# Attention over two heads at a time in a four-layer block: zero-padded keys, one list of head pairs per layer, fewer passes in stick-breaking

## The chip, the cores and the metric

One core of one Trainium2 chip runs the whole program in one launch. The metric is device microseconds of that core: 2575.2 as the median of three runs (2564.73 to 2580.36). One execution was profiled; it took 2568.69 us, and the span from its first to its last instruction is 2566.9 us.

Words used below: TensorE does matrix products (PE in rows; its weight loads are PEld), VectorE is DVE, ScalarE is ACT, GpSimd is POOL, SyncE is SP. A matrix product takes a stationary operand (up to 128 rows by 128 columns) and streams a moving operand through it. A float32 product is recorded as two matmuls, a transpose as one.

## The reference

256 tokens of width 1024 pass through two blocks of two layers. All arithmetic is float32. The parts that the change touches are the attentions of three of the layers. In the first layer eight heads do stick-breaking attention and eight do dilated attention; for 256 tokens the dilated branches come together in one bias row per head:

```python
z = jnp.einsum('bqhd,bkhd->bhqk', q_blk, k) * scale
causal = k_pos[None, :] < (start + jnp.arange(Q_BLOCK))[:, None]
log_keep = jnp.where(causal, jax.nn.log_sigmoid(-z), 0.0)
later = lax.cumsum(log_keep, axis=3, reverse=True) - log_keep
log_w = jnp.where(causal, jax.nn.log_sigmoid(z) + later, -jnp.inf)
return jnp.einsum('bhqk,bkhd->bqhd', jnp.exp(log_w), v)
```

The third layer has three softmax attentions over 256 keys (selected blocks, window, block mixture, here "moba"; eight heads of width 64 each), the fourth has one of four heads of width 128 + 64 ("mla") and one of eight heads of width 64 with a sink ("sliding"). Each of them is

```python
s = jnp.einsum('bkgqd,bksd->bkgqs', qb, k_w) * scale + bias
p = e / (jnp.sum(e, axis=-1, keepdims=True) + ...)   # e = exp(s - max)
o = jnp.einsum('bkgqs,bksd->bkgqd', p, v_w)
```

Everything else (feed-forward, mixture of experts, mLSTM, projections) stays as it is.

## The kernel before

The program is a list of stages (`STAGES`), and each engine walks through the list with its own function for each kind of stage. Between most stages all engines drain and wait for each other (`boundary`); stages in `JOINED` run into each other, the softmax attentions of one layer among them. Inside a stage the order on each engine is the order of the code, and semaphores with constant counts tie the engines together. Nothing is planned or reordered.

Weights come in pieces of 1 MB into a ring of five buffers, issued by SP. ACT rounds each piece to a high part (`high_part`), DVE subtracts it to get the low part, and TensorE does three products for each. The first one or two pieces of the stage after next are split `early`, inside the attention.

Queries and keys lie transposed in `big`, two heads to a block of 256 columns: one head in rows 0 to 63, the other in rows 64 to 127. A head's scores are causal, so for the first 128 queries only 128 keys are computed and for the second 128 queries all 256: 384 columns for each head, in `wide[:, 0, h, :]`.

**Softmax attention** (`soft_attention`), for each head h, one after the other:
- TensorE: two float32 products of 64 rows, 128 and 256 columns moving, into bank h % 2 (line 847 in rows, since all products go through one helper); three transposes of the exponentials (line 1052); three products with the values (64 columns moving, stationary `PT`).
- DVE (`biased_scores`, lines 2038 and 2042): scale and bias for 384 columns out of the bank, then the row maximum of each query tile; later the copy of the transposed exponentials out of the bank to `PT[h % 2]` (line 2056).
- ACT: two exponentials with their row sums (line 1633).

On TensorE's queue head h's transposes come first, then the scores of head h + 2, then the values of head h - 1. At the end of a stage DVE divides by the sums (and multiplies by the gates) out of banks 4 and 5 into `nrm`; where the next stage is an attention too, its first two heads' scores are biased before that.

**Stick-breaking** (`stick`) keeps the scores of a head the other way round (keys on partitions). For eight heads each: DVE copies the scores out of the bank; ACT does Abs and Exp, and after the eighth head Ln; DVE then does three passes over 384 columns (max and add; subtract; multiply by the strict causal mask), all 24 before it does anything else; TensorE sums over later keys with a constant triangle and a block of ones (`later`: 256, 128 and 128 columns moving); DVE subtracts, ACT exponentiates, DVE multiplies by the mask again, and TensorE multiplies with the values.

Of the kernel before, what the change touches and what calls it, by code (L numbers as in the profile page):

```python
# [38 lines left out]
ALU = mybir.AluOpType  # L39
# [43 lines left out]
C_MINCL = C_MSTRICT + W3  # L83
# [12 lines left out]
def shape_constants():  # L96
# [3 lines left out]
    for at, mask in ((C_MSTRICT, j > p), (C_MINCL, j >= p)):  # L100
# [40 lines left out]
def build(nc, I, out):  # L141

    ctx = ExitStack()
    with ctx:
# [83 lines left out]
        p_read = sem("p_read")  # L228
# [123 lines left out]
        def wide_at(at, n):  # L352
# [9 lines left out]
        S_RW, S_R = 232, 360  # L362

# [19 lines left out]
        QA, KA, VA, QD, KD, VD = (1024 * i for i in range(6))  # L383
        M_PRE, M_V = 0, 4096
        (N_Q, N_KC, N_VC, N_KS, N_VS, N_KW, N_VW, N_QB, N_KB, N_VB) = (
            0, 1024, 1280, 1536, 1792, 2048, 2304, 2560, 3584, 4608)
# [12 lines left out]
        def t2(at, scale=1.0):  # L399
            return [("TT", 0, 256, big[:, at:at + 512], scale)]  # L400

# [13 lines left out]
        def gview(at):  # L415
# [3 lines left out]
            "attn": [t2(QA, 0.125), t2(QA + 512, 0.125), t2(KA), t2(KA + 512), n256(VA, 512, 0), n256(VA, 512, 1),  # L419
                     t2(QD, 0.125), t2(QD + 512, 0.125), t2(KD), t2(KD + 512), n256(VD, 512, 0), n256(VD, 512, 1)],  # L420
# [6 lines left out]
                     [("T", 0, P, big_t(N_KS, 0), 1.0), n1(big_n(N_VS, P), P)],  # L427
                     [("T", 0, P, big_t(N_KW, 0), 1.0), n1(big_n(N_VW, P), P)],
                     [n1(gview(S_G))],
                     t2(N_QB, 0.125), t2(N_QB + 512, 0.125), t2(N_KB), t2(N_KB + 512),  # L430
# [3 lines left out]
                    [("T", 0, P, big_t(O_K, 0), 1.0), n1(big_n(O_V, P), P)]],  # L434
# [7 lines left out]
        def pair_heads(qat, kat):  # L442

            def parts(h):
                p0 = 64 * (h % 2)
                return [(big[p0:p0 + 64, qat + (h // 2) * T:qat + (h // 2 + 1) * T],
                         big[p0:p0 + 64, kat + (h // 2) * T:kat + (h // 2 + 1) * T])]
            return parts

        def group_heads(qat, kat):  # L450

            def parts(h):
                p0, g = 64 * (h // 4), h % 4
                return [(big[p0:p0 + 64, qat + g * T:qat + (g + 1) * T], big[p0:p0 + 64, kat:kat + T])]
            return parts

        def mla_heads(h):
            qrT = aux[0:64, A_QRT + h * T:A_QRT + (h + 1) * T]
            return [(big_t(O_QNT, h), big_t(O_KNT, h)), (qrT, aux[0:64, A_KRT:A_KRT + T])]
# [3 lines left out]
        def soft(parts, v, heads, dv, dst, bias=True, scale=1.0, pad=None, gate=None):  # L463
            return dict(parts=parts, v=v, heads=heads, dv=dv, dst=dst, bias=bias, scale=scale, pad=pad, gate=gate)

        SOFT = {
            "dilated": soft(pair_heads(QD, KD), lambda h, t: big_n(VD, 512)[:, t, 64 * h:64 * h + 64], H, 64, 512),
            "selected": soft(group_heads(N_Q, N_KS), lambda h, t: big_n(N_VS, P)[:, t, 64 * (h // 4):64 * (h // 4) + 64],
                             H, 64, 0, gate=1),
            "window": soft(group_heads(N_Q, N_KW), lambda h, t: big_n(N_VW, P)[:, t, 64 * (h // 4):64 * (h // 4) + 64],  # L470
                           H, 64, 0, gate=2, pad=S_PAD),
            "moba": soft(pair_heads(N_QB, N_KB), lambda h, t: big_n(N_VB, 512)[:, t, 64 * h:64 * h + 64], H, 64, 512),
# [6 lines left out]
        for spec in SOFT.values():  # L479
            spec["head0"], spec["step0"], spec["steps"] = at, steps, 3 if spec["pad"] is None else 5  # L480
            at, steps = at + spec["heads"], steps + spec["heads"] * spec["steps"]
# [1913 lines left out]
```

## Time and profile before

| | |
|---|---|
| median of three runs | 2575.2 us |
| profiled execution | 2568.69 us, span 2566.9 us |
| TensorE busy, share of the span | 2257.0 us, 88% |
| mean granted TensorE clock | 0.893 of full speed |
| stick-breaking (first score product to last copy) | 311.6 to 358.7 us |
| dilated attention | 358.8 to 391.2 us |
| selected, window, moba | 1393.2 to 1488.3 us |
| mla, sliding | 2033.1 to 2090.0 us |

The stages are told apart by the lines of their rows. The granted clock is shown as a share of 2.4 GHz; two levels occur, 1.0 and 0.5 (1.2 GHz). A row of the view by stretches gives each engine's busy time and count, then the clock and the DMA share.

### The profile page before, as it was taken

The page shows a single profiled execution, that of the slowest core. Times are in us where ns is not written, and L with a number is a line of the kernel's source. Part 1 is how long each engine was busy: PE and PEld are TensorE (multiplying, and loading weights), DVE is VectorE, ACT ScalarE, POOL GpSimd, SP SyncE. Part 2 cuts the span into 40 slices and gives each one's busy share as a digit, 9 for nine tenths or more (in the row PEclk, how much of TensorE's full clock was granted, in tenths as well). Part 3 has the DMA queues.
Part 4 walks back from the last instruction along what each step waited for, and adds up shares of the span by engine and source line. Part 5 has one row for each costly group of instructions (what it writes and reads, how often), then busy time and mean ns, then how long its engine had stood idle before and what let it go on. Part 6 is the DMA issues. An engine that isn't in the chain of part 4 may idle for free.

```text
span 2566.9 us, 31115 instructions
## 1 busy us (share of the span) xinstructions
PE 2257.0 (88%) x13152; PEld 1966.7 (77%) x13152; DVE 1731.5 (67%) x1455; ACT 1067.0 (42%) x1078; POOL 694.8 (27%) x340
## 2 busy tenths in 40 slices
PE   7997968998998955899897977999997886999996
PEld 6897957997997954899795666877776675877775
DVE  5896355997998446699622556777776256777766
ACT  4433434334334324333321234555553223555554
POOL 2996002995996000499300000000000000000000
PEclk9998958998999976999896578999998777999998
DMA  9775504776776530578551004887775203777873
GB/s 331 262 266 202 174 1 145 269 264 216 264 264 219 165 100 9 197 259 281 185 154 60 1 30 160 302 284 272 276 266 174 66 1 116 254 270 266 297 259 145
DMA packets 281915, 495.91 MB, mean 193 GB/s; under 512 B 11816, under 2 KB 167576, under 8 KB 281744
## 3 DMA queue, kind: packets, MB, share of 16 engines
q1 hardware_dynamic: 257952, 410.13, 47.7%
q0 software_dynamic: 23552, 82.75, 9.0%
q8 instruction: 104, 1.70, 0.3%
q10 hardware_dynamic: 272, 1.05, 0.1%
q14 instruction: 35, 0.29, 0.0%
HBM read 486.50 MB, written 12.10 MB: 194 GB/s over the span
## 4 chain that ended last, share of the span: by engine, by line
PE 75%; DVE 13%; DMA 5%; ACT 4%; issue 2%; DVEq 0%; ACTq 0%; SPq 0%
PE psum L847 73%; DVE low L1757 3%; DMA ring<-in_moe_w_up 3%; ACT wh L1440 2%; DVE nrm L1757 1%; PE psum L1052 1%; DMA ring<-in_ffn_w_up 1%; DVE wide L1757 1%; PE psum L904 1%; DVE xl L1757 1%; DMA ring<-in_ffn_w_gate 1%; DVE wide L2126 1%; DVE hl L1757 1%; DVE nrm L1816 1%; DVE nrm L1991 1%
## 5 line engine op out<-in xcount | busy, mean ns | idle before, releaser
L1757 DVE TENSOR_TENSOR low<-ring,wh 128x2048 fp32r<-128x2048 f32 x386 | 1075.8, 2807 | 371.2 <-ACT wh L1440 369.1
L1440 ACT ACTIVATE wh<-ring 128x2048 fp32r<-128x2048 f32 x386 | 733.4, 1906 | 691.8 <-PE psum L847 282.0
L847 PE MATMUL psum<-xh,wh 128*128 128x256 f32 x1832 | 523.6, 286 | 20.3 <-DVEq L580 18.5
L847 PE MATMUL psum<-xh,low 128*128 128x256 f32 x1832 | 524.4, 286 | 0.0
L847 PE MATMUL psum<-xl,wh 128*128 128x256 f32 x1832 | 521.9, 285 | 0.0
L847 PEld LDWEIGHTS psum<-xh,wh 128*128 128x128 f32 x1832 | 354.4, 193 | 26.6 <-DVEq L580 20.9
L665 POOL TENSOR_TENSOR big<-big 128x1024 f32<-128x1024 f32 x144 | 366.8, 2547 | 11.3
L847 PEld LDWEIGHTS psum<-xl,wh 128*128 128x128 f32 x1832 | 353.3, 193 | 1.6
L847 PEld LDWEIGHTS psum<-xh,low 128*128 128x128 f32 x1832 | 353.4, 193 | 0.0
L847 PE MATMUL psum<-wh,xh 128*128 128x256 f32 (+5 forms) x864 | 279.3, 323 | 14.2 <-DVEq L580 8.8
L847 PE MATMUL psum<-wh,xl 128*128 128x256 f32 (+5 forms) x864 | 276.0, 319 | 0.0
L847 PE MATMUL psum<-low,xh 128*128 128x256 f32 (+5 forms) x864 | 275.8, 319 | 0.0
L847 PE MATMUL psum<-wh,hh 128*128 128x512 f32 x672 | 268.3, 399 | 7.7 <-DVE low L1757 7.7
L847 PE MATMUL psum<-wh,bigr 128*128 128x512 f32 x768 | 251.7, 402 | 16.6 <-DVE hl L1757 16.6
L847 PE MATMUL psum<-wh,hl 128*128 128x512 f32 x672 | 266.0, 396 | 0.0
L847 PE MATMUL psum<-low,hh 128*128 128x512 f32 x672 | 265.9, 396 | 0.0
L634 POOL DMA_DIRECT2D gain<-adaln_parts x12 | 6.4, 538 | 879.6 <-DVE nrm L1757 827.5
L665 POOL TENSOR_TENSOR big<-big,ccol 128x2048 f32<-128x2048 f32 x48 | 195.9, 4081 | 40.4 <-DMA big<-in_ada_w 39.3
L847 PEld LDWEIGHTS psum<-wh,xh 128*128 128x128 f32 x864 | 169.2, 196 | 27.6 <-DVEq L580 10.8
L847 PEld LDWEIGHTS psum<-wh,bigr 128*128 128x128 f32 x768 | 145.8, 190 | 55.0 <-DVE low L1757 21.9
L847 PEld LDWEIGHTS psum<-wh,xl 128*128 128x128 f32 x864 | 168.8, 195 | 11.9
L847 PEld LDWEIGHTS psum<-low,xh 128*128 128x128 f32 x864 | 169.6, 196 | 10.7
(318 smaller groups left out, 2645.5 us busy)
## 6 DMA issues: line engine op xcount, KB each, us to landing
ring<-in_moe_w_gate SPq DMA_DIRECT2D x64, 1024.0 KB, 5.2
ring<-in_moe_w_up SPq DMA_DIRECT2D x64, 1024.0 KB, 5.3
ring<-in_moe_w_down SPq DMA_DIRECT2D x64, 1024.0 KB, 5.0
big<-in_ada_w POOLq DMA_DIRECT2D x48, 1024.0 KB, 6.6
ring<-in_ffn_w_gate SPq DMA_DIRECT2D x44, 1024.0 KB, 5.4
ring<-in_ffn_w_up SPq DMA_DIRECT2D x44, 1024.0 KB, 5.7
ring<-in_ffn_w_down SPq DMA_DIRECT2D x44, 1024.0 KB, 5.2
ring<-in_mlstm_w_in SPq DMA_DIRECT2D x16, 1024.0 KB, 5.6
```

The source lines that it names most:

```text
L634: pool.dma_start(gain[k % GAINBUFS][:, :], src).then_inc(gain_in[k % GAINBUFS], 16)
L665: pool.tensor_tensor(out_, a, b, op).then_inc(ada_step, 1)
L847: return pe.matmul(out_, lhsT, rhs, start=start, stop=stop, **kw)
L904: last = pe.transpose(psum[:, q, i * P:(i + 1) * P], nrm[:, t, f:f + P], ident)
L1052: last = pe.transpose(psum[:, 2 + h % 2, i * P:(i + 1) * P], wide[:, 0, h, i * P:(i + 1) * P], ident)
L1440: act.activation(wh[n % PARTS][:, 0:w], ring[n % RING][:, 0:w], ACT.Copy).then_inc(high, 1)
L1757: return dve.tensor_tensor(out_, a, b, op)
L1816: ins = dve.scalar_tensor_tensor(out=nrm[:, t, :], in0=x[:, t, :], scalar=stat[:, t:t + 1], in1=gain[g % GAINBUFS][:, :], op0=ALU.mult, op ...
L1991: ins = dve.scalar_tensor_tensor(out=nrm[:, t, :], in0=y, scalar=stat[:, t:t + 1], in1=factor, op0=ALU.mult, op1=ALU.mult)
L2126: dve.scalar_tensor_tensor(out=cv[:, m, tap:T], in0=src[:, 0:T - tap], scalar=w, in1=cv[:, m, tap:T], op0=ALU.mult, op1=ALU.add)\
```

## The change

Two heads are handled together everywhere in the attentions.

- **Padded keys.** ACT writes the transposed keys (for stick-breaking the queries) of two heads into a tile of 512 columns: head one in rows 0 to 63 of the first 256 columns, head two in rows 64 to 127 of the second 256, zeros elsewhere. GpSimd writes the zeros (`pad_keys`) when the projection stage begins. Such a projection piece takes two ACT copies of 64 partitions instead of one of 128 (kind "Z"). One float32 product with the stationary queries of both heads on 128 rows then gives the scores of both heads: 512 columns moving for the second query tile, 256 for the first.
- **Pairs.** DVE biases both heads in two operations (512 and 256 elements in each row) and takes the maxima in two. ACT does four exponentials for a pair, then itself copies the first head's transposed exponentials to `PT[0]`; DVE copies the second's to `PT[1]`. TensorE's order is: six transposes of the pair, scores of the pair after next, values of the pair.
- **One list per layer.** Selected, window and moba become one stage, mla and sliding one; scores of the next attention start while the last pairs of the previous one run. Maxima and sums have two sets of columns that alternate. The division of an attention follows on DVE behind the biasing of the pair after next.
- **Early pieces.** ACT splits them before the exponentials of the last pair (before: behind the fourth head of eight), DVE behind the last copy, as before.
- **Stick-breaking.** The strict mask is added to the scores as 0 or -1e30 when they leave the bank, so both multiplications by the mask go. The triangle now includes the diagonal, so the separate subtraction goes. Copies, Abs, Exp, Ln and max-and-add work on two heads (768 elements).

```diff
+    c[:, C_MSTRICT:C_MSTRICT + P] = (j > p)[:, :P]
+    for at, mask in ((C_STICK, np.where(j > p, 0, NEG)), (C_MINCL, j >= p)):
...
-    c[:, C_AFTER:C_AFTER + P] = p > j[:, :P]
+    c[:, C_AFTER:C_AFTER + P] = p >= j[:, :P]
...
+        def pair_heads(qat, keys):
+
+            def products(p, t):
+                q, n = big[:, qat + p * T + t * P:qat + p * T + (t + 1) * P], (t + 1) * P
+                return [(0, 2 * n, q, padded(keys, p)[:, :, 0:n], True, True)]
+            return products
...
-                for name in ("selected", "window", "moba"):
-                    add("soft", name)
+                add("soft", ("selected", "window", "moba"))
...
+            def pad_keys(tile):
+
+                tile = tile.rearrange("p (n h t) -> p n h t", h=2, t=T)
+                for half in range(2):
+                    pool.memset(tile[64 * half:64 * half + 64, :, 1 - half, :], 0.0).then_inc(zeroed, 1)
...
+                for i, pair in enumerate(run):
+                    turn_probs(*pair, 0)
+                    turn_probs(*pair, 1)
+                    if i + 2 < len(run):
+                        scores_read(*pair)
+                        scores(*run[i + 2])
+                    values(*pair, 0)
+                    values(*pair, 1)
...
+                        elif kind == "Z":
+                            n = m // P
+                            both_ = dst.rearrange("p (j h t) -> p j h t", j=n, h=2)
+                            src = psum[:, b, at:at + n * T].rearrange("p (j t) -> p j t", j=n)
+                            act.activation(both_[0:64, :, 0, :], src[0:64], ACT.Copy, scale=scale)
+                            dst, src = both_[64:P, :, 1, :], src[64:P]
...
+                for i, (name, p) in enumerate(run):
+                    a = SOFT[name]
+                    j = a["pair0"] + p
+                    act.wait_ge(biased, a["step0"] + a["steps"] * (p + 1))
+                    for h in a["pair"](p):
+                        for t, (lo, hi) in ((1, (P, W3)), (0, (0, P))):
...
+                    act.wait_ge(p_turned, 2 * j + 1)
+                    if j:
+                        act.wait_ge(headout, 2 * j - 1)
+                    act.activation(PT[0][:, :], psum[:, 2, 0:W3], ACT.Copy).then_inc(p_read_act, 1)
...
+                    if i == len(run) - 2:
                         for j, shape in enumerate(early(s + 2)):
                             high_part(PIECE0[s] + j, shape)
...
             def stick(s, k):
 
+                for p in range(H // 2):
+                    dve.wait_ge(stick_pe, p + 1)
+                    for lo, hi, bank in ((0, T, p % 2), (T, W3, 6 + p % 2)):
+                        tt(wide[:, 0, 2 * p:2 * p + 2, lo:hi],
+                           psum[:, bank, 0:2 * (hi - lo)].rearrange("p (h w) -> p h w", h=2),
+                           spread(const[:, C_STICK + lo:C_STICK + hi], 1, 2), ALU.add).then_inc(stick_dve, 1)
+                for p in range(H // 2):
+                    z, sp = (wide[:, i, 2 * p:2 * p + 2, :] for i in range(2))
+                    dve.wait_ge(stick_act, p + 1)
+                    dve.scalar_tensor_tensor(out=sp, in0=z, scalar=0.0, in1=sp, op0=ALU.max, op1=ALU.add)\
+                        .then_inc(stick_dve, 1)
                 for h in range(H):
-                    dve.wait_ge(stick_pe, h + 1)
-                    dve.tensor_copy(wide[:, 0, h, :], psum[:, h % 2, 0:W3]).then_inc(stick_dve, 1)
-                for h in range(H):
-                    z, sp_h = wide[:, 0, h, :], wide[:, 1, h, :]
-                    at = H + 3 * h
-                    dve.wait_ge(stick_act, h + 1)
-                    mark(dve.scalar_tensor_tensor(out=sp_h, in0=z, scalar=0.0, in1=sp_h, op0=ALU.max, op1=ALU.add),
-                         stick_dve, at + 1)
-                    mark(tt(z, z, sp_h, ALU.subtract), stick_dve, at + 2)
-                    mark(tt(sp_h, sp_h, const[:, C_MSTRICT:C_MSTRICT + W3], ALU.mult), stick_dve, at + 3)
...
+                for i, (name, p) in enumerate(run):
+                    j = SOFT[name]["pair0"] + p
+                    dve.wait_ge(p_turned, 2 * j + 2)
+                    if j:
+                        dve.wait_ge(headout, 2 * j)
+                    dve.tensor_copy(PT[1][:, :], psum[:, 3, 0:W3]).then_inc(p_read_dve, 1)
+                    if i + 2 < len(run):
+                        biased_scores(*run[i + 2])
+                    if i == len(run) - 1:
+                        for j, shape in enumerate(early(s + 2)):
+                            low_part(s, PIECE0[s] + j, shape)
+                    if p == SOFT[name]["pairs"] - 1:
+                        scaled_values(name)
```

**TensorE in the middle of the dilated attention.** Before, two heads (`PT0` and `PT1` are the transposed exponentials; `psum<-big` without `PT` are scores, `psum<-const,wide` transposes):

```order
L1052 MATMUL psum<-const,wide 128x128 x3
L847 MATMUL psum<-big 128x128
L847 MATMUL psum<-big 128x256
L847 MATMUL psum<-big,PT0 128x64 x3
L1052 MATMUL psum<-const,wide 128x128 x3
L847 MATMUL psum<-big 128x128
L847 MATMUL psum<-big 128x256
L847 MATMUL psum<-big,PT1 128x64 x3
```

Now, the same work of one pair:

```order
L1094 MATMUL psum<-const,wide 128x128 x6
L889 MATMUL psum<-big 128x512
L889 MATMUL psum<-big 128x256
L889 MATMUL psum<-big,PT0 128x64 x3
L889 MATMUL psum<-big,PT1 128x64 x3
```

Four score products have become two of double width; transposes and values are as many as before, and each kind stands together.

**DVE in stick-breaking.** Before (the triple of lines 2017 and 1757 stands eight times):

```order
L2012 COPY wide<-psum 128x384 x8
L2017 SCALAR_TENSOR_TENSOR wide<-wide 128x384
L1757 TENSOR_TENSOR wide<-wide 128x384
L1757 TENSOR_TENSOR wide<-wide,const 128x384
...
L1757 TENSOR_TENSOR wide<-wide,psum 128x384 x8
L1757 TENSOR_TENSOR wide<-wide,const 128x384 x8
```

Now (the first two rows stand four times):

```order
L1818 TENSOR_TENSOR wide<-psum,const 128x2x256
L1818 TENSOR_TENSOR wide<-psum,const 128x2x128
...
L2080 SCALAR_TENSOR_TENSOR wide<-wide 128x768 x4
L1818 TENSOR_TENSOR wide<-wide,psum 128x384 x8
L2100 SCALAR_TENSOR_TENSOR wide<-psum,biasT 128x2x256
L2100 SCALAR_TENSOR_TENSOR wide<-psum,biasT 128x2x128
```

Of the 24 operations between the logarithms and the subtractions four are left, and none stands between the subtractions and the values.

**ACT at the end of the dilated attention.** Now, the last two pairs (`wh1<-ring0` is the early high part):

```order
L1696 ACTIVATE PT0<-psum 128x384
L1486 ACTIVATE wh1<-ring0 128x2048
L1691 ACTIVATE wide,small<-wide,small 128x256
L1691 ACTIVATE wide,small<-wide,small 128x128
L1691 ACTIVATE wide,small<-wide,small 128x256
L1691 ACTIVATE wide,small<-wide,small 128x128
L1696 ACTIVATE PT0<-psum 128x384
```

The high part stands ahead of the last pair's four exponentials; before it stood ahead of the fifth head's.

## Rows read from the trace of the kernel before

**Rows 1.** Page, busy time of each engine and share of the span.

```profile
PE 2257.0 (88%) x13152; PEld 1966.7 (77%) x13152; DVE 1731.5 (67%) x1455; ACT 1067.0 (42%) x1078; POOL 694.8 (27%) x340
```

**Rows 2.** By stretches: length, busy PE, PEld, DVE, ACT, POOL, then PEclk, DMA.

```profile
340.30:343.90 3.60, 3.60 (x13) 3.23 (x14) 0.86 (x2) 1.39 (x3) 0.00 (x0) 0.50 0.00 0
344.10:347.70 3.60, 3.60 (x24) 3.25 (x23) 2.19 (x4) 1.83 (x4) 0.00 (x0) 1.00 0.02 5
348.90:350.80 1.90, 1.90 (x17) 1.90 (x18) 1.90 (x5) 0.00 (x0) 0.00 (x0) 1.00 0.00 0
...
358.80:391.20 32.40, 27.93 (x104) 20.82 (x104) 18.23 (x36) 9.69 (x33) 0.00 (x0) 0.50 0.00 1
391.30:394.90 3.60, 3.60 (x16) 3.22 (x16) 1.55 (x3) 1.79 (x3) 0.00 (x0) 0.50 0.00 0
395.30:396.30 1.00, 0.00 (x0) 0.00 (x0) 0.82 (x2) 0.26 (x1) 0.00 (x0) 1.00 0.00 0
...
1393.20:1488.30 95.10, 86.44 (x312) 64.66 (x312) 56.12 (x131) 25.69 (x98) 0.00 (x0) 0.50 0.00 1
...
2033.20:2050.70 17.50, 17.39 (x46) 10.42 (x47) 5.79 (x14) 4.43 (x14) 0.00 (x0) 0.51 0.00 0
2051.10:2054.10 3.00, 3.00 (x16) 2.97 (x15) 1.20 (x3) 0.41 (x2) 0.00 (x0) 0.50 0.00 0
2054.20:2060.90 6.70, 4.07 (x26) 2.92 (x25) 4.43 (x13) 1.97 (x8) 0.00 (x0) 1.00 0.00 0
2061.00:2090.00 29.00, 23.52 (x89) 17.98 (x86) 19.99 (x46) 9.62 (x27) 0.00 (x0) 0.50 0.00 1
```

**Rows 3.** Timeline of TensorE in the dilated attention: start, length, what.

```profile
373.64 1.65 PE L847 MATMUL psum<-big 64*128 64x128 f32 x4
375.22 1.54 PE L847 MATMUL psum<-big,PT 128*128 128x64 f32 x6
376.55 0.85 PE L1052 MATMUL psum<-const,wide 128*128 128x128 f32 x3
...
377.33 1.65 PE L847 MATMUL psum<-big 64*128 64x128 f32 x4
```

**Rows 4.** Timeline of TensorE where the sliding attention begins.

```profile
2055.07 1.57 PE L847 MATMUL psum<-big 64*128 64x128 f32 x8
...
2058.92 0.55 PE L1052 MATMUL psum<-const,wide 128*128 128x128 f32 x3 [2.27 <-ACT wide L1633]
```

**Rows 5.** Timeline of TensorE: transposes of two heads in a row of mla.

```profile
2040.48 0.90 PE L1052 MATMUL psum<-const,wide 128*128 128x128 f32 x3
...
2044.76 0.90 PE L1052 MATMUL psum<-const,wide 128*128 128x128 f32 x3
```

**Rows 6.** Timeline of stick-breaking, ACT, DVE and TensorE.

```profile
324.71 4.15 ACT L1619 ACTIVATE wide<-wide,const 128x384 f32<-128x384 f32 x8
325.36 0.56 DVE L2017 SCALAR_TENSOR_TENSOR wide<-wide 128x384 f32<-128x384 f32 x1 [7.01 <-ACT wide L1619]
...
340.29 7.46 PE L847 MATMUL psum<-wide,const 128*128 128x256 f32 x36 [9.53 <-DVE wide L1757]
...
357.62 1.09 ACT L1625 ACTIVATE nrm<-psum 128x512 f32<-128x512 f32 x2 [8.72 <-PE psum L847]
```

**Rows 7.** Groups by form, dilated attention: busy, mean ns of one.

```profile
L2038 DVE SCALAR_TENSOR_TENSOR wide<-psum,biasT 128x384 f32<-128x384 f32 x8 | 4.5, 558 | 18.3 <-PE psum L847 18.3
...
L1633 ACT ACTIVATE wide<-wide,small 128x256 f32<-128x256 f32 x8 | 3.9, 492 | 0.0
L2042 DVE TENSOR_REDUCE small<-wide 128x1 f32<-128x256 f32 x8 | 3.4, 420 | 0.3
...
L1757 DVE TENSOR_TENSOR low<-ring,wh 128x2048 fp32r<-128x2048 f32 x1 | 2.3, 2282 | 0.0
L1440 ACT ACTIVATE wh<-ring 128x2048 fp32r<-128x2048 f32 x1 | 1.9, 1893 | 0.0
L1757 DVE TENSOR_TENSOR nrm<-psum,small 128x512 f32<-128x512 f32 x2 | 1.3, 687 | 0.0
```

More of the change, by code:

```diff
@@ L461, in build, with soft @@
         vmla = big_n(O_KVM, 1024).rearrange("p t (h w) -> p t h w", h=MH)
-        def soft(parts, v, heads, dv, dst, bias=True, scale=1.0, pad=None, gate=None):
-            return dict(parts=parts, v=v, heads=heads, dv=dv, dst=dst, bias=bias, scale=scale, pad=pad, gate=gate)
+        def soft(products, pair, v, heads, dv, dst, bias=True, scale=1.0, pad=None, gate=None):
+            return dict(products=products, pair=pair, v=v, heads=heads, pairs=heads // 2, dv=dv, dst=dst, bias=bias,
+                        scale=scale, pad=pad, gate=gate)
@@ L473, in build @@
-            "mla": soft(mla_heads, lambda h, t: vmla[:, t, h, P:2 * P], MH, P, 0, bias=False, scale=192.0 ** -0.5),
-            "sliding": soft(group_heads(O_Q, O_K), lambda h, t: big_n(O_V, P)[:, t, 64 * (h // 4):64 * (h // 4) + 64],
+            "dilated": soft(pair_heads(QD, big[:, KD:KD + 2048]), next_to,
+                            lambda h, t: big_n(VD, 512)[:, t, 64 * h:64 * h + 64], H, 64, 512),
+            "selected": soft(group_heads(N_Q, big[:, N_KS:N_KS + 512]), across,
+                             lambda h, t: big_n(N_VS, P)[:, t, 64 * (h // 4):64 * (h // 4) + 64], H, 64, 0, gate=1),
@@ L478, in build, with pairs_of @@
         at, steps = 0, 0
-        for spec in SOFT.values():
-            spec["head0"], spec["step0"], spec["steps"] = at, steps, 3 if spec["pad"] is None else 5
-            at, steps = at + spec["heads"], steps + spec["heads"] * spec["steps"]
+        for i, spec in enumerate(SOFT.values()):
+            spec["index"], spec["pair0"], spec["step0"], spec["steps"] = i, at, steps, 4 if spec["pad"] is None else 5
+            spec["nmx"], spec["sum"], spec["inv"] = (S_SOFT[i % 2] + 16 * j for j in range(3))
+            at, steps = at + spec["pairs"], steps + spec["pairs"] * spec["steps"]
+        def pairs_of(names):
+            return [(name, p) for name in names for p in range(SOFT[name]["pairs"])]
         STAGES = []
@@ L1075, in gates @@
+                pe.wait_ge(zeroed, {"dilated": 4, "selected": 8, "mla": 10}[names[0]])
+                scores(*run[0])
+                scores(*run[1])
+                for i, pair in enumerate(run):
[6 more added lines that the diff above has]
+                    values(*pair, 1)
             def gates(s, k):
@@ L1622, in stick @@
+                for p in range(H // 2):
+                    sp = wide[:, 1, 2 * p:2 * p + 2, :]
+                    act.activation(sp, sp, ACT.Ln, bias=ones).then_inc(stick_act, 1)
+                for h in range(H):
+                    act.wait_ge(stick_dve, H + H // 2 + h + 1)
                     act.activation(wide[:, 0, h, :], wide[:, 0, h, :], ACT.Exp).then_inc(stick_act, 1)
-                act.wait_ge(stick_pe, 2 * H + 1)
+                act.wait_ge(stick_pe, H // 2 + H + 1)
                 for t in range(TT):
@@ new lines, in biased_scores @@
+                ha, hb = a["pair"](p)
+                hs = slice(ha, hb + 1, hb - ha)
+                nmx = small[:, a["nmx"]:a["nmx"] + 16].rearrange("p (h t) -> p h t", t=TT)
+                dve.wait_ge(score, j + 1)
+                tiles = ((1, P, W3, j % 2), (0, 0, P, 6 + j % 2))
+                for t, lo, hi, bank in tiles:
+                    add = biasT[:, hs, lo:hi] if a["bias"] else spread(const[:, C_CAUSAL + lo:C_CAUSAL + hi], 1, 2)
+                    dve.scalar_tensor_tensor(out=wide[:, 0, hs, lo:hi],
+                                             in0=psum[:, bank, 0:2 * (hi - lo)].rearrange("p (h w) -> p h w", h=2),
+                                             scalar=a["scale"], in1=add, op0=ALU.mult, op1=ALU.add).then_inc(biased, 1)
```

289 lines of the change are left out of this document (135 added, 154 removed).

## The prediction

> **What bounds the kernel now.** I read the page first: TensorE is busy for 88% of the span and no other engine comes near [rows 1], so only a change that shortens TensorE's work, speeds its clock or fills its gaps counts. Then the view by stretches. The three softmax stages and stick-breaking (47.1 us from first product to last copy) take 231.6 of 2566.9 us. In the dilated stage TensorE is busy for 27.93 of 32.40 us, in the third layer's for 86.44 of 95.10, and the granted clock is 0.50 in both from end to end, that is 1.2 GHz; DVE is busy for 18.23 and 56.12 [rows 2]. So these stages are bound by a TensorE at half speed. In the timeline a head takes 3.69 us (373.64 to 377.33): 1.58 for the scores, 1.33 for the values, 0.78 for the transposes, handovers included [rows 3].
>
> **Why the clock is low.** Rises follow stretches in which products on 128 rows stand back to back: `later` ran 3.60 us at 0.50 and then 3.60 at 1.00; the 16 transposes behind the dilated stage ran at 0.50, and the next microsecond, with no matmul in it, already has 1.00; mla's last values and transposes (128 rows, 3.00 us full) at 0.50 are followed by 6.70 us at 1.00 [rows 2]. The stages of 64-row scores never rise, although TensorE is as busy, and even mla, whose scores are half 128 and half 64 rows, stays at 0.51 for 17.50 us with 17.39 busy. So rows count, and transposes count. Values (64 columns per load) kept 1.00 right behind `later` for the 1.90 us shown.
>
> The Trainium skill, page "TensorE: Matmul & The Clock Gate", speaks against this twice. Its section on the HAM clock gate lets the clock follow how busy TensorE has been; by that alone padding to 128 rows changes nothing. This trace disagrees: 86.44 of 95.10 us busy never lifted the clock. Its Part 4 says that transposes do not count as busy. This trace disagrees here too (the 16 transposes). By the page the softmax stages would stay at half speed, which is rival B.
>
> **The change part by part**, from the bottom up.
>
> *One pair at full clock.* Scores: as many columns as two heads have now, and those took 1.57 us at 1.00 [rows 4]. Values: 17 records in 1.90 us, 0.112 each [rows 2]; 12 make 1.34. Transposes: 0.55 for three [rows 4], three more at 0.112: 0.88. One further handover, 0.1. Sum 3.9 us, where two heads take 7.37 now. *At half clock:* scores 2 x 1.58, values 2 x 1.33, transposes 2 x 0.78 [rows 3], less a handover of some 0.3 saved at two places: 6.9. Which clock holds: six transposes and the scores of a pair now stand together, all on 128 rows, 4.2 us at half speed with one handover in it, as in the stretches after which it rose. Once up, a pair has its 128-row work in 3.8 of 3.9 us. I take full clock.
>
> *Do DVE and ACT keep up with 3.9?* DVE for a pair: bias 0.69 (512 elements as in the division) and about 0.43, maxima 0.69 and 0.42, a copy of 0.56 [rows 7]: 2.8. ACT: four exponentials, at most 0.49 each [rows 7], and the copy, 0.52 by the logarithms' 4.15 / 8 [rows 6]: 2.5 to 3. Yes, in both cases; the waiting work (bias of pair i + 2 behind the copy of pair i) has almost a whole period before it is needed. The padded attentions add some 0.35 on DVE; it still fits.
>
> *Fill and tail.* First transposes of a stage end after its first scores (1.6), bias and maxima (2.2), exponentials (2.0) and transposes (0.4): 6.2. Behind the last transposes: copy 0.56, early low part 2.28, division 2 x 0.69 [rows 7], small steps and waits 0.4: 4.6, as today. New on the path: the early high part, 1.89 [rows 7], stands ahead of the last pair's exponentials; about 0.5 is covered, so +1.4.
>
> *Dilated*, four pairs: 6.2 + 3 x 3.9 + 1.4 + 4.6 = 23.9, and 0.9 for a start that may still be at half clock: 24.8 for 32.4. **-7.6.**
>
> *Selected, window, moba*, twelve pairs: 6.2 + 11 x 3.9 + 1.4 + 4.6 = 55.1. First scores start at half clock: +0.7. At two crossings DVE divides and gates (four operations of 0.69 and small ones, 3.2) before it copies for the next pair; its slack is 1.1: +2.1 each. Sum 60.0 for 95.1. **-35.1.** The crossings themselves cost now too (their gain is in the 95.1).
>
> *mla, sliding* (2033.1 to 2090.0, 57 us). An mla head takes 4.28 from transposes to transposes, 3.8 of it scores [rows 5]: they still have 64-row halves. Both mla pairs' scores now come first: 4 x 3.8 = 15.2, at half clock. Then transposes, sliding's first scores and mla's values, all on 128 rows: 7.0 at half clock, the clock rising on the way: 5.6. The second such group at full clock: 4.0. Three periods of sliding 11.7 (the last two without scores: -0.6), its transposes 0.7; two high parts on ACT: +3.0; tail with two low parts and the sink's steps: 7.2. Sum 46.8. **-10.2.**
>
> *Stick-breaking.* The first logarithm starts at about 324 as now: four pairs of Abs and Exp at 2 x 0.87 (0.52 for 384 elements; 768 by the slope to 1.89 for 2048 [rows 6, 7]) save 1.9, wider scores and mask additions give 1.0 of it back. Then today 24 operations (first at 325.36) stand ahead of the subtractions, and `later` runs from 340.29 [rows 6]. Now four of 0.96 do, and `later` starts at 325.7 and can run through: about 2.4 heads at 1.71 (half clock, twice 0.925) until the clock rises, 5.6 at 0.925 (today 3.60 us for 3.9 heads [rows 2]): 9.2, to 334.9. Values follow at once, without the mask pass: 48 records, 5.4 at full clock; today 8.7. End 340.6, copies 1.1 [rows 6]: 341.7 for 358.7, -17.0. If the clock falls in the values they take 10.2, and it is -12.2. I take **-16.5**.
>
> *At nothing or nearly.* GpSimd's zeros: its queue stands empty of urgent work when a projection begins, and the first scores come over 60 us later in both large stages; price if the cover goes, a few us once. The second copy of a padded piece: 0.6 on ACT, which has 2.5 us of work per projection piece against over 5 on TensorE; only the last piece of the fourth layer shows: +0.5.
>
> Sum: -7.6 - 35.1 - 10.2 - 16.5 + 0.5 = -68.9. From the profiled 2568.7: 2499.8. That execution lies 6.5 us under the median of 2575.2 and inside the three runs' own spread; I forecast **2500 us**, 2.9% less than the median.
>
> **Rivals.**
>
> *A. The clock holds only in part, or handovers are dearer* (a pair takes 5.2). For it: mla rose late and fell back when 64-row scores and waits came [rows 2]; crossings leave TensorE waiting for 2 us. Against: the 128-row share of a pair. 22 pairs x 1.3 = +28.6: 2528. 12%.
>
> *B. The clock stays at 0.50 in the softmax stages* (the zeros, or the page's rule). Against it: the moving operand of the 16 transposes is the identity, nearly all zeros, and it lifted the clock. 22 x (7.37 - 6.9) = 10 less fills and the high parts, some 6; stick-breaking -13 to -16.5: 2548. 10%.
>
> *C. Slower than before: the pair turns serial.* ACT now carries exponentials and a copy, and the copy of pair i waits for transposes that wait for its own exponentials; if nothing overlaps at half clock, a pair is 2.0 (exponentials) + 1.3 + 0.9 (copies) + 2.9 + 2.7 = 9.8. 22 x 2.4 = +53, less 16.5: 2605. It decides from a pair of 7.37 + 16.5 / 22 = 8.1 us on. Against: scores of pair i + 2 lie between the transposes and values on TensorE's queue and need nothing fresh. 3%.
>
> *Forecast*, 75%: 2484 (pairs at 3.6, handovers wholly hidden, and the values at full clock) to 2515 (values at half clock, every fill a few us longer).
>
> The range takes the forecast's and most of A: **2482 to 2534**. A change of 1% (25.8 us) is about what can be told here; B lies on that line (2549.4), so half of it is "same": faster 0.92, same 0.05, slower 0.03.
>
> **What the changed profile would show.** The clock at 1.00 from the second pair of each softmax list on; scores starting every 3.9 us in the dilated stage; DVE's two copies no longer behind 24 passes, `later` starting near 326; the third layer's attention at about 60 us. The forecast is wrong if the stretches of 128-row scores still read 0.50, or if TensorE waits on ACT's copy (line 1696) in every pair.

## The result, and the profile after

The changed kernel takes **2495.3 us** (median of four runs, 2489.99 to 2501.18) against 2573.4 (four runs): a ratio of 0.970, 95% interval 0.966 to 0.973. The forecast was 2500 and its range 2482 to 2534, so the result lies inside. The profiled execution took 2491.27 us, its span 2489.5 at a mean granted clock of 0.922; before it was 2566.9 at 0.893. One line of the page answers to [rows 1]:

```profile
PE 2186.2 (88%) x13056; PEld 1909.5 (77%) x13056; DVE 1692.1 (68%) x1337; ACT 1075.1 (43%) x1097; POOL 703.5 (28%) x350
```

TensorE lost 70.8 us of busy time with only 96 fewer matmuls, so most of it is the same work at another speed. The view by stretches has the four attention stages (stick-breaking, dilated, selected to moba, mla and sliding) and the first score products of mla alone; the columns are those of [rows 2]:

```profile
312.25:342.81 30.56, 20.63 (x113) 16.93 (x113) 12.00 (x20) 19.27 (x25) 0.00 (x0) 0.83 0.11 35
342.81:365.79 22.98, 16.84 (x88) 12.51 (x89) 13.56 (x24) 10.63 (x37) 0.00 (x0) 0.84 0.00 1
...
1366.74:1423.98 57.24, 47.64 (x264) 36.23 (x264) 40.22 (x83) 29.09 (x110) 0.00 (x0) 0.86 0.00 1
1965.79:2009.93 44.14, 36.06 (x156) 25.27 (x156) 22.90 (x45) 18.98 (x58) 0.00 (x0) 0.70 0.00 1
1965.79:1980.47 14.68, 14.68 (x33) 7.85 (x34) 1.94 (x4) 3.15 (x9) 0.00 (x0) 0.51 0.00 1
```

The clock was 0.50 throughout the dilated and the third layer's attention before, and 0.50 in mla and sliding but for one stretch of 6.7 us; now it is 0.84, 0.86 and 0.70. The timeline of TensorE in the dilated stage (start, length, what) answers to [rows 3]:

```profile
353.00 0.83 PE L1094 MATMUL psum<-const,wide 128*128 128x128 f32 x6
353.66 1.46 PE L889 MATMUL psum<-big 128*128 128x512 f32 x4
354.95 1.45 PE L889 MATMUL psum<-big,PT 128*128 128x64 f32 x12
356.23 0.82 PE L1094 MATMUL psum<-const,wide 128*128 128x128 f32 x6
...
359.98 0.55 PE L1094 MATMUL psum<-const,wide 128*128 128x128 f32 x3 [1.12 <-ACT wide L1691]
```

From one pair's transposes to the next it is 3.23 us. The last row shows the last pair: its transposes wait 1.12 us for exponentials, which stand behind the early high part on ACT. Stick-breaking, against [rows 6], ACT's logarithms and then TensorE's sums and values:

```profile
324.59 3.41 ACT L1674 ACTIVATE wide<-wide,const 128x768 f32<-128x768 f32 x4
...
326.57 9.74 PE L889 MATMUL psum<-wide,const 128*128 128x256 f32 x48 [8.73 <-DVE wide L2080]
336.14 5.47 PE L889 MATMUL psum<-big,wide 128*128 128x64 f32 x48
```

The first of the two crossings in the third layer, in the chain of waits:

```profile
1380.80 2.58 PE psum L889 x16
1383.38 0.66 PE psum L1094 x6
1384.04 1.31 PE psum L889 x4
...
1385.37 1.02 DVE wide L2100 x2
1386.39 0.93 DVE small L2105 x2
...
1390.82 1.52 PE psum L889 x12
```

The chain leaves TensorE for DVE (biasing, maxima, the division and gating) and comes back at 1390.82. Then the clock is gone for a while; TensorE's timeline at the same place:

```profile
1390.82 1.52 PE L889 MATMUL psum<-big,PT 128*128 128x64 f32 x12 [2.25 <-DVE nrm L1818]
...
1392.90 2.76 PE L889 MATMUL psum<-big 128*128 128x512 f32 x4
```

The scores that took 1.46 take 2.76: the granted clock is 0.50 from 1392.77 to 1396.18. The second crossing looks the same, with a wait of 2.46 and scores of 2.77.

By stages, each from its transposes of the normed tokens to the next: projection, stick-breaking and dilated 157.12 to 131.71, the third layer's 231.85 to 193.98, the fourth's 133.33 to 121.34. These are 75.3 of the 77.4 us that the span lost. All others move by less than 2.3 us, but for the last (the second mixture of experts and the end), whose instructions are the same: 435.34 before, 439.63 after.

### The profile page after: what moved, and what is told of

It reads as the page before. It is cut to its first block, busy times and chain, and to the rows that moved or that the text cites. A ratio compares the mean times of both kernels' runs of the same rounds, so it can differ in the third digit from the quotient of the medians.

```text
span 2489.5 us, 30826 instructions
## 1 busy us (share of the span) xinstructions
PE 2186.2 (88%) x13056; PEld 1909.5 (77%) x13056; DVE 1692.1 (68%) x1337; ACT 1075.1 (43%) x1097; POOL 703.5 (28%) x350
## 4 chain that ended last, share of the span: by engine, by line
PE 75%; DVE 12%; DMA 5%; ACT 4%; issue 2%; DVEq 1%; ACTq 0%; SPq 0%
PE psum L889 73%; DVE low L1818 3%; DMA ring<-in_moe_w_up 3%; ACT wh L1486 2%; DVE nrm L1818 1%; DMA ring<-in_ffn_w_up 1%; DVE xl L1818 1%; DVE wide L2188 1%; DMA ring<-in_ffn_w_gate 1%; PE psum L946 1%; DVE hl L1818 1%; DVE nrm L1877 1%; PE psum L1094 1%; DVE nrm L2052 1%; DVEq L611 0%
```

## The experiments

**Theory T**: products on 128 rows lift the granted clock, and this is most of the gain in the softmax stages. **Rival P**: pairing and the joined list keep TensorE fed, and that is the gain. In stick-breaking, T holds DVE's queue of passes responsible. "Stage" below is the length by the same marks as just above, which the profile of each kernel gives. In the first two kernels the scores are not those of the heads, as their expectations say; their order and shapes are what is compared.

### Pairs, but 64 rows (e1_rows64, e1_again)

```diff
-                return [(0, 2 * n, q, padded(keys, p)[:, :, 0:n], True, True)]
+                return [(i * n, i * n + n, q[0:64], padded(keys, p)[0:64, 0, 0:n], True, True)
+                        for i in range(2)]
```

> The changed kernel, but the scores of a pair of heads come from two products on 64 rows each instead of one on 128 (the same columns, the same order, pairs and lists; the second head of a pair gets the first head's keys and queries, so its scores are the wrong ones). Theory T (the 128 rows lift the clock, and the clock is most of the gain): the granted clock of the dilated stage and of the third layer's attention reads 0.50 through most of it, a pair takes 6.3 to 6.9 us instead of 3.24; 18 pairs by about 3.3 is +60 (mla and sliding +5 at most): 2550 to 2565 us. Rival P (pairing, fewer operations and the joined list give the gain, and the clock would rise for any TensorE kept this busy): the clock stays at 1.00 and the time within 10 us of the changed kernel's 2495.

Measured: 2521.2 us (ratio to before 0.981, 0.979 to 0.983). By stretches, the third layer's attention, and TensorE's chain in it:

```profile
1373.52:1459.00 85.48, 82.97 (x312) 71.23 (x313) 40.70 (x83) 28.89 (x110) 0.00 (x0) 0.50 0.00 1
```

```profile
1400.75 1.28 PE psum L1096 x6
1402.03 5.61 PE psum L891 x20
1407.63 1.28 PE psum L1096 x6
```

In this layer T holds where it spoke of the clock: 0.50 from end to end, and 6.89 us a pair; the dilated attention reads 0.53. TensorE was busy for 82.97 of 85.48 us, a larger share than in the changed kernel (47.64 of 57.24), and it stayed at half speed. P falls. The Trainium skill, page "TensorE: Matmul & The Clock Gate", Part 1, lets the clock follow how busy TensorE has been recently; the measurement disagrees again, and it decides.

My figure for the whole was wrong: 2550 to 2565 expected. The stage of the third layer costs +28.2 (222.22), the dilated one +5.9, where eleven and three periods of 3.65 more would be 40 and 11. I had forgotten what the changed kernel pays and this one doesn't: TensorE stands idle for 2.5 us in this attention against 9.6, so at 6.89 a pair most of DVE's work at a crossing and of ACT's high part is hidden, and a clock that is low cannot fall. And 13 us lay elsewhere: the last stage, untouched, took 426.61 instead of 439.63. So I ran the same kernel again:

> The kernel with two 64-row products for a pair's scores once more, for its last stage alone: it took 426.61 us without one drop of the clock. If that belongs to the program, it is 427 again and the whole about 2520; if it is chance, 435 to 445 and the whole 2530 to 2538.

It took 2529.97 (one execution). The third layer's stage is 222.25, within 0.03 us of the first execution, and the dilated one 137.07 (137.59). The fourth layer's does not repeat, 117.11 against 128.03, nor does the last stage, 440.76; more on it below.

The fourth layer also shows where T stops. Its sliding attention has 64-row scores in this kernel too, and there they ran at full clock (the second execution):

```profile
2020.35:2033.50 13.15, 12.83 (x95) 11.33 (x93) 10.59 (x26) 8.36 (x29) 0.00 (x0) 1.00 0.01 1
```

```profile
2024.04 0.82 PE L1096 MATMUL psum<-const,wide 128*128 128x128 f32 x6
2024.79 1.57 PE L891 MATMUL psum<-wide,big 64*128 64x256 f32 x8
2026.43 1.52 PE L891 MATMUL psum<-big,PT 128*128 128x64 f32 x12
2027.79 0.82 PE L1096 MATMUL psum<-const,wide 128*128 128x128 f32 x6
```

A pair takes 3.75 us here, not 6.89. The clock had been at 1.00 since 1993.46, through mla; in the first execution it rose in the middle of this list, at 2027.51. So rows decide the clock in the dilated and the third layer's attention, but 64-row scores as such do not rule out full speed. What is different in the fourth layer was not tried.

### One head at a time, but 128 rows (e2_before_rows128)

```diff
-                p0 = 64 * (h % 2)
-                return [(big[p0:p0 + 64, qat + (h // 2) * T:qat + (h // 2 + 1) * T],
-                         big[p0:p0 + 64, kat + (h // 2) * T:kat + (h // 2 + 1) * T])]
+                return [(big[:, qat + (h // 2) * T:qat + (h // 2 + 1) * T],
+                         big[:, kat + (h // 2) * T:kat + (h // 2 + 1) * T])]
```

> The kernel before, one head at a time, but the scores of a head in dilated, selected, window, moba and sliding come from a product on all 128 rows of the two heads' block (so each holds the sum of two heads' scores; same columns, same number of instructions, no zeros needed). Theory T: rows alone lift the clock; the stages go to 1.00, a head then takes 2.0 us by TensorE and up to 2.3 where DVE or ACT (three operations and two exponentials a head) are slower, instead of 3.7: the third layer's attention 95 falls to 55 to 65, dilated 32.5 to 21 to 25; time 2505 to 2530 us. Rival P (pairs are needed, because the handovers inside a head keep the clock down): clock 0.50, 2565 to 2580 us.

Measured: 2530.0 us (0.984, 0.982 to 0.985), at the upper end; the third layer's attention, 70.10, lies above the 55 to 65 expected. The dilated attention and the third layer's:

```profile
359.55:382.68 23.13, 16.66 (x105) 13.11 (x105) 17.84 (x36) 9.57 (x33) 0.00 (x0) 0.93 0.00 1
1384.53:1454.63 70.10, 53.30 (x313) 43.30 (x313) 55.16 (x131) 25.57 (x98) 0.00 (x0) 0.84 0.00 1
```

Rows alone bring the dilated attention from 32.47 to 23.13; the changed kernel has 22.98. In the third layer they bring 25.0 of the 37.9 us. This is the cleanest experiment on T: order, columns and counts are those of the kernel before, and only the rows differ. Of the 12.9 us that are missing in the third layer, DVE has a part: it is busy for 55.16 of 70.10 us (40.22 in pairs), and TensorE waits for its copy of the transposed exponentials 12 times, 7.6 us in all. The joined list, which this kernel lacks, has another; the two are not told apart here. Pairs and list without rows (the kernel above) are worth 9.6. So the two parts together give 3.3 us more than their sum.

### Without the crossings (e8_no_crossing)

```diff
-                    if i + 2 < len(run):
+                    if i + 2 < len(run) and run[i + 2][0] == pair[0]:
...
+                    if i + 2 < len(run) and run[i + 1][0] != pair[0]:
+                        scores_read(*pair)
+                        scores(*run[i + 1])
+                        scores(*run[i + 2])
```

(and the same on DVE: biasing of the next two pairs, then the division).

> The changed kernel without the crossing of attentions: the first two score products of the next attention stand behind the last values of the one before, and DVE biases its first two pairs and then divides, as in the kernel before. If the joined list is worth what I put it at (a crossing costs 2.1 us instead of a fill of 6.2 and a division): 4 to 6 us more at each of the three crossings, and the clock falls in each gap: +12 to +22 in all, the third layer's attention at 66 to 72 us. Rival (the list is worth little, since the crossings already stop TensorE for 2 us and cost the clock): under +6.

Measured: 2503.8 us, +8.5; the third layer's stage 200.40, +6.4 for two crossings. Neither forecast is met: +12 to +22 was too much, under +6 too little. TensorE's timeline behind the last pair of an attention:

```profile
1390.20 0.55 PE L1094 MATMUL psum<-const,wide 128*128 128x128 f32 x3 [2.03 <-ACT wide L1695]
...
1394.49 1.52 PE L889 MATMUL psum<-big,PT 128*128 128x64 f32 x12 [1.57 <-DVE nrm L1822]
```

A fill here is a wait of 2.03 and one of 1.57, and the scores between are at full clock. I had gone by the 6.2 of a fill from a stage's start, but the scores in it are work that is due in either order. Counted from the start of the list, the seventh pair's transposes come 1.5 us later than in the changed kernel, so this crossing costs 1.5 more. The second costs the other 4.9; there the clock is 0.50 for 10.2 us, from 1410.32 on, against 3.4 in the changed kernel. So the rival had part of the reason (a crossing already costs a wait and some clock), and what a fill costs hangs on whether the clock falls.

### What a crossing and the high part cost (e3_adds_later, e4_high_early, e5_both)

```diff
-                        link(tt(part, y, f, ALU.mult))
-                        dve.wait_ge(scaled, 2 * a["index"])
-                        tt(o, o, part, ALU.add).then_inc(scaled, 1)
+                        tt(part, y, f, ALU.mult).then_inc(scaled, 1)
...
+                    if p < TT and i > p and SOFT[run[i - p - 1][0]]["gate"] is not None:
+                        added_values(run[i - p - 1][0], p)
```

> The changed kernel, but where one gated attention hands over to the next DVE only multiplies out of banks 4 and 5 at once; the two additions to nrm (0.69 each) follow behind the biasing of the next two pairs. Theory T (the wait of 2.25 us ahead of the values at 1390.82 is DVE's queue: biasing, four passes of 0.69, then the copy): the wait falls by 1.4 us at each of the two crossings of the third layer, to about 0.8, and if the clock then does not fall behind it (2.76 us for scores that take 1.46), another 1.5 each: that layer's attention 57.2 falls to 51 to 54.5; -3 to -6 in all. Rival (the additions only move: they delay the copy of a later pair by as much): within 1 us.

The third layer's stage fell from 193.98 to 187.67, -6.3, a little more than expected. At the first crossing:

```profile
1387.18 1.46 PE L889 MATMUL psum<-big 128*128 128x512 f32 x4
1389.43 1.52 PE L889 MATMUL psum<-big,PT 128*128 128x64 f32 x12 [0.79 <-DVE wide L1818]
1390.79 0.82 PE L1094 MATMUL psum<-const,wide 128*128 128x128 f32 x6
1391.45 1.46 PE L889 MATMUL psum<-big 128*128 128x512 f32 x4
```

The wait is 0.79 instead of 2.25 (1.00 instead of 2.46 at the second crossing), and the next scores take 1.46 instead of 2.76. Two additions of 0.69 taken off the path of each crossing paid twice, since the clock did not fall. The program as a whole took 2494.4 us, no better than the changed kernel: the first mixture of experts, also untouched, took 431.98 instead of 424.94.

```diff
-                    if i == len(run) - 2:
+                    if i == 0:
```

> The changed kernel, but ACT splits the early weight pieces behind the first pair of a list instead of ahead of the last pair's exponentials. Theory T (the high part of 1.9 us holds up the last pair: a gap of 1.1 us before its transposes in the dilated stage): -1.1 in dilated and about as much in the third layer, -2 to -3 in the fourth where it is 3.7 us; -4 to -6 in all. Rival (ACT is no freer in the first pair, and the high part delays the second pair's exponentials instead; or DVE's low part and the division set the end anyway): within 1 us, or up to +2.

2492.0 us, -3.3 by the medians where 4 to 6 less were expected. The third layer's stage is -1.2, as expected. The dilated one (with its projection and stick-breaking) is 130.28 instead of 131.71, but the unchanged program came to 130.29 when it ran again (below), so the stage decides nothing. The dilated attention alone takes 21.24 against 22.98 and 22.70; but it took 21.40 in the kernels without crossings and with eight masks, which leave it as it is. So only the wait that is gone is shown, not what it is worth in time. In the fourth layer the whole stage says nothing either (118.01, against 121.34 and 117.62 unchanged), but the list from its first transposes on does: 27.59, and 27.58 and 27.59 in the two executions below, where five executions with the old order took 29.53 to 30.47. Its last pair, in the changed kernel and then here:

```profile
2001.15 1.78 PE L1094 MATMUL psum<-const,wide 128*128 128x128 f32 x6 [2.87 <-ACT wide L1691]
```

```profile
2001.76 1.05 PE L1094 MATMUL psum<-const,wide 128*128 128x128 f32 x6
```

> Both of these edits, additions later and high parts early. If both theories hold: the dilated stage 22 us, the third layer's attention 50 to 53.5, mla and sliding 41 to 42.5; -7 to -11 in all, 2485 to 2490 us. If neither: as the changed kernel, about 2495.

2484.1 us (0.963, 0.959 to 0.967), just below the expected 2485 to 2490. Then once more, beside the changed kernel on one chip, five rounds:

> Additions later and high parts early, once more beside the changed kernel: 8 to 12 us less than it by the medians seen so far (2484.1 against 2495.3); by the stages alone 13 us less (2.8 dilated, 7.2 third layer, 3.3 fourth), of which the last stage may take up to 6 back.

> The changed kernel itself, as a yardstick for the version with both edits on the same chip: 2490 to 2500 us. Its last stage (from its transposes of the normed tokens on) took 439.63 us with four drops of the clock in it; if that length belongs to the program, it is within 1 us of that again; if it depends on how the stage happens to lie against the stretches in which the clock is set, it comes out anywhere between 427 and 446.

2491.6 us (2484.27 to 2494.83) against 2497.8 (2493.33 to 2501.66). This version beats both kernels: by 6.2 us over the change on the same chip, less than the 8 to 12 expected, and by 11.2 against the first measurement of the change. The third layer's stage was 193.98 and 193.97 for the change, 186.78 and 186.74 for this: -7.2, as expected. The fourth layer's gave nothing in the last pair of runs (121.87 against 117.62, for a reason given below), and the untouched first mixture of experts took 433.60 against 427.68. The dilated attention took 21.10 and 20.98. Its last pair's transposes (at 359.04) no longer wait for exponentials:

```profile
356.57 0.83 PE L1094 MATMUL psum<-const,wide 128*128 128x128 f32 x6
357.65 1.55 PE L889 MATMUL psum<-big,PT 128*128 128x64 f32 x12 [0.25 <-ACT PT L1696]
359.04 0.91 PE L1094 MATMUL psum<-const,wide 128*128 128x128 f32 x6
```

### Stick-breaking: the passes (e6_16_passes, e7_8_masks)

```diff
-                    dve.scalar_tensor_tensor(out=sp, in0=z, scalar=0.0, in1=sp, op0=ALU.max, op1=ALU.add)\
-                        .then_inc(stick_dve, 1)
+                    ins = dve.scalar_tensor_tensor(out=sp, in0=z, scalar=0.0, in1=sp, op0=ALU.max, op1=ALU.add)
+                    for h in (2 * p, 2 * p + 1):
+                        for _ in range(2):
+                            link(ins)
+                            sp_h = wide[:, 1, h, :]
+                            ins = tt(sp_h, sp_h, const[:, C_MINCL:C_MINCL + W3], ALU.mult)
+                    ins.then_inc(stick_dve, 1)
```

> The changed kernel with 16 further passes over 384 columns on DVE in stick-breaking (two per head on the softplus, a multiplication by the inclusive mask that changes nothing), placed between the max-and-add of each pair and the subtractions, where the kernel before had its 16. Theory T (DVE's queue held the sums over later keys back by their length): 16 x about 0.45 on the stage less what lies under the logarithms; the stage takes 37 to 40 us instead of 30.56: +6 to +9. Rival: these passes were hidden, and the 16.6 us of the stage came from the wider copies, Abs, Exp and from the clock: under +2.

2502.8 us, +7.6 by the medians, and +9.4 by the stage (141.15 against 131.71), just above the range. Stick-breaking by itself takes 41.39 instead of 30.56, +10.8; the projection ahead of it and the dilated attention behind it came out 0.7 shorter each. DVE and TensorE:

```profile
335.22 0.95 DVE L2080 SCALAR_TENSOR_TENSOR wide<-wide 128x768 f32<-128x768 f32 x1
...
339.15 7.93 PE L889 MATMUL psum<-wide,const 128*128 128x256 f32 x36 [6.49 <-DVE wide L1818]
```

The max-and-add of the last pair comes at 335.22, behind twelve of the added passes, where it was over by 329.1; the values start at 346.92 instead of 336.14 (0.6 of it a shift of the whole stage). The queue of passes did hold the sums back. Part of the 10.8 is clock: it stays at 0.50 until 343.93 here, and rose at 331.22 in the changed kernel, whose sums run through.

```diff
-                    pe.wait_ge(stick_act, H // 2 + h + 1)
+                    pe.wait_ge(stick_dve, H + H // 2 + H + h + 1)
...
+                for h in range(H):
+                    dve.wait_ge(stick_act, H // 2 + h + 1)
+                    tt(wide[:, 0, h, :], wide[:, 0, h, :], const[:, C_MINCL:C_MINCL + W3], ALU.mult)\
+                        .then_inc(stick_dve, 1)
```

> The changed kernel with the eight multiplications by a mask (the inclusive one, which changes nothing) put back behind the last exponentials of stick-breaking, and the values waiting for them. If only the wait costs: the first values +1.3 us, then TensorE (0.68 us a head) is slower than DVE (0.42 to 0.55), so +1.3 in all. If the gap also lowers the clock under the values, as in the kernel before (8.7 us for values that take 5.47 now): +3.5 to +5.5. Rival: the multiplications are hidden behind the subtractions and nothing moves, under +0.5.

2494.7 us, nothing by the medians. But the gap is there:

```profile
337.79 3.83 DVE L1818 TENSOR_TENSOR wide<-wide,const 128x384 f32<-128x384 f32 x8
...
338.39 5.57 PE L889 MATMUL psum<-big,wide 128*128 128x64 f32 x48 [1.12 <-DVE wide L1818]
```

The stage begins 0.68 us later in this execution, so of the 2.25 between 338.39 and 336.14 some 1.6 are left, and the values run at full clock (5.57 for 48). The second case (a fall under the values) did not happen. Stick-breaking takes 32.06, +1.5. The dilated attention gave that back, with 21.40: its clock stays at 1.00 up to 363.05, where the changed kernel has 3.4 us at 0.50 from 348.29 on. It owes this to no mask: the kernel without crossings, whose stick-breaking and dilated attention are the changed kernel's own, also had 21.40, at 1.00 throughout. The same instructions with the same wait of 1.92 us before the first transposes met a fall of the clock in one execution and none in another.

## Why the prediction was right

**The clock** was the step that mattered, and in the dilated and the third layer's attention it held for the reason given: 128 rows lift it, one head or two, and with 64 it stayed low though TensorE was 97% busy. As a rule for every stage ("The stages of 64-row scores never rise") the reason went too far: sliding's 64-row pairs ran at 1.00 in both executions of the kernel with 64 rows. Rival B fell; rival C too, as TensorE waits for ACT's copy only in a list's last pairs, for 0.25. Of rival A the mechanism is there (the clock falls at the crossings), at a pair of 3.24, not 5.2.

**One pair: 3.9 forecast, 3.24 measured.** The scores and the first three transposes were read as the length of a row; but a row's end is modelled and overlaps the next row. From start to start the scores are 1.29 (1.57 forecast), the values 1.28 (1.34), the transposes 0.66 (0.88), and the handover of 0.1 is in them. At half clock, where I had gone by whole heads, the forecast of 6.9 met 6.89 in the kernel with 64 rows.

**Selected, window, moba: -35.1 forecast, -37.9 measured.** Eleven periods at 3.24 save 7.3 against the forecast. The crossings gave 3 to 4 back: the wait is 2.25 where I said 2.1, but I left out that the clock falls behind it, some 1.5 each. The rest, about 1, is not told apart. So two errors of opposite sign made the term look better than it was; that part is luck.

**Dilated: -7.6 and -9.5.** Three shorter periods (2.0) are the difference. But six executions of these same instructions took 21.40 to 23.04, so the term is good to 1.6 us. Of the high part, forecast at +1.4, the waits of 1.12 and 0.33 are seen in the rows; its price in time is not shown here (1.2 in the third layer).

**mla, sliding: -10.2 and -12.8.** The scores of both mla pairs take 14.68 at half clock (15.2 forecast), then the clock rises, as said. That is the common way, with 13.7 to 15.0 us in nine of the eleven executions in which these products are the changed kernel's, but not the only one. In the second execution of the changed kernel the same scores ran at full clock, in 8.72 us:

```profile
1972.01:1980.73 8.72, 8.42 (x32) 4.73 (x33) 2.19 (x5) 2.33 (x6) 0.00 (x0) 1.00 0.01 2
```

The attention took 39.08 there instead of 44.14, and so -17.9 against the one profile of the kernel before. It was the same in the kernel with 64 rows (14.82 and 8.72), and that is the largest part of why the fourth layer's stage does not repeat. What decides between the two was not tried.

**Stick-breaking: -16.5 and -16.6.** `later` starts at 326.57 (325.7), the values at 336.14 (334.9) and take 5.47 (5.4). The kernel before did not start `later` at 340.29, as the prediction has it, but at 327.16, with 12 of its 48 records; the 36 others stood behind the queue. The sum stays right, since it counts from the new start. By the stretch of stick-breaking alone the 16 passes are worth 10.8 of it and the 8 masks 1.5, and of the other 4.3 the values, 8.72 before and 5.47 now, can be 3.3; no run holds the clock there alone. Three figures of this part don't come out as written: 0.52 and 0.87 save 1.4, not 1.9; half of full clock is 1.85 a head where the rows show 1.71; and 334.9 and 5.4 make 340.3, not 340.6. Each is about 0.5 us or less.

**Copies: +0.5 forecast, nothing shown.** The first layer's projection up to the first scores took 78.16 against 77.47, but 77.42 in the changed kernel's second execution; the third layer's took the same before and after. The zeros on GpSimd were never waited for. Together 76 where 68.9 was forecast; the shorter pair is most of the difference. The last stage took 4.3 back in the profiled execution, by nothing that the change does.

## What to carry to other kernels

Look at the granted clock beside the busy share first: a TensorE that is 97% busy on 64 rows ran at half speed in the third layer, and zero padding to 128 rows, which adds no columns, doubled it. Once it is at full speed, a wait of some 2 us can be paid for twice, the wait itself and the slow stretch behind it (at the crossings it was; in other places the same wait cost no clock), so work that nobody waits for (additions, roundings) is to be moved off the few places where TensorE starves. And judge an edit of a few us by its own stretch in the trace, and by more than one execution: the third layer's stage repeats within 0.2 us, the fourth layer's differs by 11 between two executions of one program.

## Seen in the hardware, not expected

The last stage runs the same instructions in all kernels, and it took 426.61 to 445.53 us in thirteen profiled executions. What goes with its length is the number of separate stretches at 0.50 in it (its first 44 us and last 20 aside):

| stretches at 0.50 | last stage, us |
|---|---|
| 0 | 426.61 |
| 2 | 435.52, 438.42 |
| 3 | 435.34, 439.05 |
| 4 | 438.12, 439.11, 439.63, 440.76 |
| 5 | 441.25, 442.35, 442.99 |
| 6 | 445.53 |

There TensorE stands idle for more than 0.8 us at seven or eight places. The view of waits over six of them, for the changed kernel and then for the one without a drop (waiting engine and line, what for, total, times, longest):

```profile
PE psum L889 <- DVE hl L1818: 8.9, 4, 2.6
PE psum L889 <- DVE xl L1818: 5.3, 2, 2.7
```

```profile
PE psum L891 <- DVE hl L1820: 5.4, 4, 1.6
PE psum L891 <- DVE xl L1820: 3.8, 2, 2.2
```

These waits end with DVE's low part of the activations (`hl`, `xl`), which in both kernels stands on DVE's queue right behind the low part of a weight piece. They are longer in the kernel whose clock falls. In order of time the wait comes first: each of the 47 stretches of the table begins in the last 1.0 us of such a wait or within 1.5 us behind it, and none of these waits is shorter than 1.80 us. But the length does not decide alone, since 31 other waits of 1.84 to 2.74 us have no fall. The changed kernel's four stretches last 13.7 us in all, which by an estimate from the two clocks costs 6.8 us, and its waits over 0.8 us add up to 17.1 against 11.8; that is 12 of the 13 us between the two. Whether a fall also makes later waits longer stays open; two executions of one program differ in this stage by 14 us. The Trainium skill, page "TensorE: Matmul & The Clock Gate", "HAM oscillation — how this bites in real kernels", describes a kernel whose clock falls at each wait for a transfer. The trace shows falls at waits too, but only at some of them (47 of the 78 that last 1.80 us or more).
